# A hybrid decoder layer on one core: LayerNorm 1's last transposes one product chain sooner, first weight part ahead of token sums, another bank order and combining order around the last down chunks

## The reference, cut to what matters

```python
mix = jnp.concatenate([y_pool, y_ml], axis=-1).astype(x.dtype) @ w_out
x1 = _layer_norm(ALPHA * x + mix, ln1_g, ln1_b)
ff = jnp.square(jax.nn.relu(x1 @ w_ff1 + b_ff1)) @ w_ff2 + b_ff2
x2 = _layer_norm(ALPHA * x1 + ff, ln2_g, ln2_b)
```

## Time and profile before

| what | value |
|---|---|
| median of three runs | 1136.58 us (1135.80 to 1137.31) |
| the profiled execution | 1137.68 us |
| its span, first to last instruction | 1134.8 us |
| TensorE busy | 1097.5 us, 97% of the span |
| VectorE, ScalarE, GpSimd busy | 58%, 43%, 8% |
| mean granted TensorE clock | 0.988 of full speed |
| DMA | 132.70 MB, 117 GB/s |

### The profile page before, as it was taken

The page is one execution under the profiler, slowest core; times in us unless marked ns, Lnnn a source line. Parts: engine busy times, 40 slices in busy tenths (PEclk is TensorE's granted clock), DMA queues, the critical chain, the costliest instruction groups (busy, mean ns, idle before and its releaser), DMA issues. The chain is left out here.

```text
span 1134.8 us, 19572 instructions
## 1 busy us (share of the span) xinstructions
PE 1097.5 (97%) x8192; PEld 1078.6 (95%) x8192; DVE 663.8 (58%) x926; ACT 489.5 (43%) x694; POOL 90.3 (8%) x110
## 2 busy tenths in 40 slices
PE   7999999999999999999999999999999999999993
PEld 5999999999978899999999999999999999999993
DVE  5522222224567566495555655557766677878876
ACT  5622424241254366665554554545453323334022
POOL 4000000010010122000000000000000000000056
PEclk9999999999999999999999999999999999999997
DMA  9211111122115553124436354468734425334212
GB/s 252 75 47 33 40 39 39 41 84 62 38 45 164 185 175 106 51 66 156 151 121 184 113 151 147 131 183 271 271 103 141 146 80 168 115 114 165 75 49 101
DMA packets 93073, 132.70 MB, mean 117 GB/s; under 512 B 5369, under 2 KB 54105, under 8 KB 92996
## 3 DMA queue, kind: packets, MB, share of 16 engines
q1 hardware_dynamic: 89452, 121.13, 33.7%
q0 software_dynamic: 3552, 10.59, 3.2%
HBM read 97.04 MB, written 34.89 MB: 116 GB/s over the span
## 5 line engine op out<-in xcount | busy, mean ns | idle before, releaser
L1666 PE MATMUL bank<-x_hi,w_hi 128*128 128x344 f32 (+1 forms) x792 | 261.7, 330 | 3.0 <-DVE x_lo L1231 1.4
L1666 PE MATMUL bank<-x_hi,w_lo 128*128 128x344 f32 (+1 forms) x792 | 254.4, 321 | 0.0
L1666 PE MATMUL bank<-x_lo,w_hi 128*128 128x344 f32 (+1 forms) x792 | 254.1, 321 | 0.0
L1666 PE MATMUL bank<-x_hi,d_lo 128*128 128x258 f32 x1000 | 231.3, 282 | 0.0
L1666 PEld LDWEIGHTS bank<-x_hi,d_lo 128*128 128x128 f32 x1000 | 171.7, 189 | 0.0
L1666 PEld LDWEIGHTS bank<-x_hi,w_hi 128*128 128x128 f32 (+1 forms) x792 | 148.4, 187 | 10.8 <-issue 3.8
L1666 PEld LDWEIGHTS bank<-x_hi,w_lo 128*128 128x128 f32 (+1 forms) x792 | 148.1, 187 | 1.3
L1666 PEld LDWEIGHTS bank<-x_lo,w_hi 128*128 128x128 f32 (+1 forms) x792 | 148.2, 187 | 1.1
L1666 PE MATMUL bank<-x_hi,s_hi 128*128 128x258 f32 x448 | 126.5, 282 | 1.8 <-DVE s_raw_lo L1359 1.8
L1666 PE MATMUL bank<-x_lo,s_hi 128*128 128x258 f32 x448 | 126.5, 282 | 0.0
L1666 PE MATMUL bank<-t_hi,s_hi 128*128 128x258 f32 x336 | 95.2, 283 | 0.0
(11 more groups left out here) (311 smaller groups left out, 2262.6 us busy)
## 6 DMA issues: line engine op xcount, KB each, us to landing
h_ops<-h_unit SPq DMA_DIRECT2D x56, 258.0 KB, 2.5
x_lo_raw<-h_ops SPq DMA_DIRECT2D x14, 1032.0 KB, 5.2
s_raw<-in_w_ff SPq DMA_DIRECT2D x14, 1024.0 KB, 7.0
w_raw<-in_w_out SPq DMA_DIRECT2D x12, 1024.0 KB, 5.1
x_lo_raw<-h_ops SPq DMA_DIRECT2D x14, 774.0 KB, 4.6
d_raw<-in_w_ff SPq DMA_DIRECT2D x9, 1024.0 KB, 7.4
w_raw<-in_w_in SPq DMA_DIRECT2D x16, 512.0 KB, 5.3
h_ops<-t_out SPq DMA_DIRECT2D x28, 258.0 KB, 5.1
```

The costliest lines, as they stand in the source:

```text
L1666: return nc.tensor.matmul(out, lhsT, rhs, start=start, stop=stop, skip_group_check=True)
```

## The change

Five things:

1. `LN1_LAST`: tile 8's second half (norm_T, x1_T, ln1_b) stands after chain c5 instead of c6.
2. ACT makes `s_hi_12` after `hidden(9)`, ahead of the third token sum's high part, instead of after `hidden(10)`.
3. DVE makes `s_lo_12` ahead of `t_lo_part(0)` and `t_lo_part(1)` instead of behind them.
4. `combine_t2` is taken apart. Its first pass (L1512) comes behind `d_add(27, 0)`, its second (`combine_t2_y`) behind all of `d_add(27, .)`; `d_add(27, .)` no longer waits for it.
5. `down_step` uses bank 3 + (m + 1) % 3, so that m0 and m1 have banks 4 and 5, m2 has bank 3. Chunk m0 waits for `d_add(27, 0)` alone and m2 for `d_add(27, 2)`, instead of m0 for all four.

```diff
-        LN1_LAST = {1: ((0, 7),), 2: ((1, 6),), 3: ((0, 8),), 4: ((1, 7),), 6: ((1, 8),)}
+        LN1_LAST = {1: ((0, 7),), 2: ((1, 6),), 3: ((0, 8),), 4: ((1, 7),), 5: ((1, 8),)}
...
                 elif i == 9:
+                    s_hi_12(at_unit(0, 0), 0)
                     act.wait_ge(t_sum, 4)
                     A(TH[2][:, :, :], TS[2][:, :, :], ACT.Copy).then_inc(t_hi, 1)
-                elif i == 10:
-                    s_hi_12(at_unit(0, 0), 0)
...
-                    if i == B22 and g == len(GROUPS) - 1:
-                        dve.wait_ge(combined, 5)
...
             def combine_t2():
                 dve.wait_ge(dn_added, add_no[NOP * 3 + 4, 3])
+                V.tensor_tensor(Z[:, 2, :, :], Z[:, 2, :, :], Z[:, 0, :, :], ALU.add).then_inc(combined, 1)
+
+            def combine_t2_y():
+                dve.wait_ge(dn_added, len(add_no))
+                dve.wait_ge(combined, 4)
                 y12 = quad(1)
-                V.tensor_tensor(Z[:, 2, :, :], Z[:, 2, :, :], Z[:, 0, :, :], ALU.add).then_inc(combined, 1)
-                dve.wait_ge(combined, 4)
                 V.tensor_tensor(y12, y12, Z[:, 2, :, :], ALU.add).then_inc(combined, 1)
...
-                y, z = Y[:, o, blk(b)], bank[3 + m % 3][:, 0:BLK]
+                y, z = Y[:, o, blk(b)], bank[3 + (m + 1) % 3][:, 0:BLK]
...
             s_sums(at_unit(0, 0), 0)
+            s_lo_12(at_unit(0, 0), 0)
             t_lo_part(0)
             t_lo_part(1)
-            s_lo_12(at_unit(0, 0), 0)
             dve.wait_ge(gemm_done, N_OUT + 12)
...
                 d_add(t, 0)
+                if i == 6 and not more:
+                    combine_t2()
...
                     elif i == 5:
                         last_h_lo(0)
-                        combine_t2()
+            combine_t2_y()
             for m in range(24):
...
                     if m == 0:
-                        pe.wait_ge(dn_added, len(add_no))
+                        pe.wait_ge(dn_added, add_no[NOP * 4 - 1, 0])
+                    elif m == 2:
+                        pe.wait_ge(dn_added, add_no[NOP * 4 - 1, 2])
                     pe.wait_ge(down_read, m + 1)
-                    split_product(bank[3 + m % 3][:, 0:BLK], lambda k: W2H[p][:, k, cs], lambda k: W2L[p][:, k, cs],
+                    split_product(bank[3 + (m + 1) % 3][:, 0:BLK], lambda k: W2H[p][:, k, cs], lambda k: W2L[p][:, k, cs],
```

## The result

The changed kernel took 1129.58 us, the median of seven runs (1127.21 to 1132.27). The kernel before, run beside it, took 1135.75 us (seven runs, 1132.78 to 1137.31). The ratio is 0.995 with an interval of 0.9938 to 0.9961, so it is faster by 4.4 to 7.0 us. The forecast was 1130.8 us.

A forecast was written before the change was run, and what follows sets the result against it. TensorE, busy 97% of the span, was taken as the bound, so only its waits and clock move the time. 1.3 + 2.0 - 0.4 + 2.9 = 5.8 us off the median 1136.58 gave 1130.8 us, range 1129.2 to 1133.3.

The forecast's parts named there:

- What bounds the kernel: TensorE, busy 97% of the span: time moves only where it waits or its clock changes.
- Tile 8 sooner: Ahead of chain c8: tile 8's low part is ready in time, so TensorE's wait goes; gain 1.3 us.
- first weight part sooner: Ahead of P1: s_lo_12 ends before P1 is due, so TensorE's wait goes; gain 2.0 us.
- 0.4 us at P3: New wait: ACT's copy of P1 stands behind the third hidden-feature store; cost 0.4 us, bounds 0 and 0.8.
- The last chunks: Chunks m0 to m8: wait and half clock at m0 go, 3.6 us, less 0.7 in two short waits; gain 2.9.
- The half clock: Behind m0's start, 1.2 GHz for 3.41 us: costs 1.5 us, gone with the idle time; may differ between runs.
- The sum: Whole kernel: 5.8 us off, giving 1130.8 us against the median.
- A: As forecast: three waits gone, two or three short ones new; 1129.6 to 1131.9 us; chance 0.63.
- C: DVE becomes the bound behind the removed waits: gain 3.8 us, 1132.8, or 1133.8 at three places; chance 0.08.
- D: Only one of three places is gained, other operands being late: 1.3 to 2.9 us, 1133.7 to 1135.3; chance 0.07.
- E: Slower: short waits at m3, m6 and P3 keep 1.2 GHz, deciding at about nine chunks in a row; chance 0.02.
- B: Waits go, but median run had no half clock, or L1493's wait brings one: gain 4.3 us, 1132.3; chance 0.20.

The follow-up runs named there:

- Edit 1 alone: Kernel before with only tile 8's norm_T, x1_T and ln1_b one chain sooner: 1133.01 us (11 runs), ratio 0.9976.
- edit 5 alone: Kernel before with only the other banks and m0 and m2 waiting for single d_adds, combine_t2 whole: 1132.68 us (12 runs), ratio 0.9973.
- second comparison: Changed kernel, unchanged, measured again beside the kernel before: 1129.56 us (5 runs), ratio 0.994.
- edits 4 and 5 alone: Kernel before with only combine_t2 taken apart and the new banks and waits of m0 and m2: 1132.72 us (11 runs), ratio 0.9976.
- the longer wait above: Kernel before plus one DVE pass of 2.3 us on a dead tile ahead of d_add(27, .): 1138.51 us (8 runs), ratio 1.0028.
- edits 2 and 3 alone: Kernel before with only s_hi_12 behind hidden(9) and s_lo_12 ahead of both t_lo_part: 1134.66 us (11 runs), ratio 0.999.
- the version with the small instruction: Changed kernel with L1287's scalar_tensor_tensor made a tensor_scalar with one tensor operand: 1130.71 us (5 runs), ratio 0.9953.
- the one after it: Changed kernel with combine_t2's second pass between d_add(27, 0) and d_add(27, 1), first pass ahead, and L1287 as tensor_scalar: 1129.15 us (6 runs), ratio 0.9935.

## Why the prediction was right, point by point

**What bounds the kernel** held: only TensorE's waits and clock moved the time.

**Tile 8 sooner, 1.3 us, and first weight part sooner, 2.0 us, less 0.4 us at P3.** Together 2.9 us, and 36.96 - 34.05 = 2.91 us measured. The sum is right and its split is wrong. The step that failed is the one that booked the 2.0 us on edits 2 and 3. The working had in hand that everything on DVE behind `ln1_b(8)` starts 3.5 us sooner, and then never asked where `s_lo_12` would end by that alone: 491.41 + 1.22 - 3.5 = 489.1, against P1 due at 489.47. Edit 1 alone shows it: both waits gone, 0.28 us in hand. P3's new wait came as worked out: it was due at 489.48 + 5.76 = 495.24 and came at 495.62, 0.38 us late, where 0.4 was taken between 0 and 0.8 (the 0.29 us in the table are less, since P1 no longer has a restart of 0.1 us behind it). In the changed kernel it is the third store that ACT waits for:

```profile
494.82 0.20 ACT L843 ACTIVATE small<-const_T 128x2 f32<-128x2 f32 x1 [0.78 <-DMA h_first<-h_blk]
494.94 0.58 ACT L846 ACTIVATE up_tmp<-bank 128x516 f32<-128x516 f32 x1
```

Edit 1 alone has the same 6.14 us from P1 to P3, so this price is that of P1's being on time, not of edits 2 and 3.

**The last chunks, 3.6 less 0.7 us.** 1.98 + 0.94 = 2.92 us measured, 2.9 forecast. The wait was 1.98 (1.99 forecast). The half clock, 1.5 forecast, is 1.55 by another comparison in which only the clock differs: m0 to m8 is 16.67 us before and 15.12 in the trace of edit 1 alone. The restart, 0.1 forecast, is 15.12 - 15.04 = 0.08, against the trace with no wait at all there. The two waits behind the moved pass, at m3 and m6, cost 15.73 - 15.04 = 0.7 us. DVE's order was as written out: `combine_t2_y` at 1057.11, `w2_lo_part(1)` right behind, and `add_down(0)` with `add_down(1)` behind that, which is what m3 waits for:

```profile
1057.11 2.31 DVE L1514 TENSOR_TENSOR y_acc<-y_acc,z_acc 128x2064 f32<-128x2064 f32 x1
1059.34 2.29 DVE L1532 TENSOR_TENSOR d_lo<-d_raw,d_lo 128x2048 fp32r<-128x2048 f32 x1
1061.54 1.05 DVE L1549 SCALAR_TENSOR_TENSOR y_acc<-bank,const_T,y_acc 128x344 f32<-128x344 f32 x2
```

What the step didn't see is that the gain needs edit 5 alone. With d_add(27, 0) the first of DVE's four and the only one that m0 waits for, m0 is 0.2 us late even with both passes ahead of it.

**The sum.** 5.8 us forecast; the spans differ by 6.8. The 1.0 us more are 0.68 at L1493, forecast to stay at 2.3 and found between 1.6 and 2.4 in the twelve traces of kernels that don't touch it, and 0.3 in small terms. It is spread, not a gain: the changed kernel run again has 2.08 us there. That the spans moved more than the sum is luck of this trace. Between the medians it is 6.2 us, by the ratio 5.7.

**The rivals.** A came, at its lower edge (1129.6 to 1131.9 forecast). C is excluded as to cause (no wait of DVE's beyond the short ones named), D too (all three waits gone), E as well; its "nine chunks in a row" are five, since a chunk of 1.88 us takes 3.76 at half clock and 18 us hold five of those.

B, that the median run of before has no half clock at m0, was priced at a gain of 4.3 us. That lies just outside the 4.4 to 7.0 us of the change and clearly outside the 5.3 to 8.2 us of its second comparison (0.9928 to 0.9953). Against it stand also edits 4 and 5 alone, which would give 1.4 us without a half clock and 2.9 with it (1.4 to 4.1 measured), and the longer wait above; the same wait of 1.8 us brought the half clock in three traces of four. All this makes B unlikely. What no run shows is the clock at m0 in the median run itself: **this stays open**.

The mean granted clocks can't settle it. Those of 35 runs of the kernel before lie at 0.985 to 0.987 (12 runs), 0.988 to 0.989 (18) and 0.991 to 0.992 (5), and the middle spans of the three groups are 1135.3, 1133.6 and 1132.1 us: steps of 1.5 to 1.7 us, about one half-clock stretch. But the mean doesn't say which stretch. Of the thirteen traces twelve have half clock near 280 us, for 3.4 or 6.8 us, eight near 370 us, five near 15 us, and all have it in the last 12 to 16 us of the span, where TensorE has nothing left to do. Both traces of before fall into the middle group, at 0.988 and 0.989, and they have not the same stretches: the first has one near 15 us, the second none.

```profile
14.53:17.94 3.41, 3.41 (x16) 2.61 (x17) 1.05 (x2) 0.93 (x2) 0.00 (x0) 0.50 1.05 291
```

```profile
13.00:17.00 4.00, 3.09 (x24) 2.42 (x25) 2.10 (x4) 1.13 (x3) 0.00 (x0) 1.00 1.04 274
```

B's second part, a half clock behind L1490 in its new place, came in neither of the two traces of the changed kernel. Of the twelve traces three have it there, for 1.4 to 1.5 us behind a wait of 1.8 to 2.4 us (edits 2 and 3 alone, the version with the small instruction, and the one after it), and the others none.

## What to carry to other kernels

When a step is moved sooner, follow its whole engine on to the next wait before a second edit is credited with removing that wait: here one number in a table did the work of three edits. Where the bound engine waits at a seam for the last of several results, let it take first the buffer that is emptied first; reordering the work around it may then bring nothing. And look upstream of each wait that is left for a store that stands in one queue behind a large load it doesn't depend on.

## What the runs showed of the hardware

**The half clock comes and goes with the same idle time.** Behind 1.8 us of TensorE's idle time ahead of m0 the granted clock stood at 0.50 for 3.4 us in three traces and at 1.00 in a fourth. Behind 1.75 us ahead of P1 it stood at 0.50 in one trace of five, and behind 1.6 to 2.4 us between the up and the down products in three of twelve. Such a stretch of 3.4 us cost 1.4 to 1.6 us. The Trainium skill, "TensorE: Matmul & The Clock Gate", section "What's actually happening", says that what the clock's monitor watches is free-running and doesn't reset when a kernel starts. The traces agree as far as they go, since equal idle time was followed by either clock; they don't show the monitor.

**A pass of POOL holds a tiny instruction of DVE.** One column took 2.38 us when it began 0.02 us behind POOL's pass, 0.16 us when it began 0.03 us ahead of it. Two that began in the middle of a pass, in the same trace of edit 5 alone, took 0.91 and 1.09 us and ended within 0.02 us of it. The form with one tensor operand and a per-partition scalar took 0.21 us each time, also when it began 0.02 us behind POOL. The Trainium skill, "SBUF — State Buffer", section "SBUF: two separate sides", says that the port pair that the two engines share is an exclusive lock and not a split of bandwidth, that the one that starts first takes it, and names DVE operations with two SBUF inputs among those that need it, against a GpSimd operation that reads SBUF. The traces agree with that rule.

**Order within one queue.** Two stores of 258 KB landed 6.9 us after their issue behind a load of 1 MB in SP's queue, and 3.1 and 4.1 us after it when they were issued ahead of that load.
